# Half of a depthwise convolution as diagonal products on TensorE, and the query norm folded into the attention scores

## The reference

```
h = concat(meta, x)                                   # 272 x 1024
for l in range(2):
    z = rms(h) @ w_in[l]                              # 18 tiles of 128 columns
    ya = attention(z)    # 8 query heads, 2 key heads of 64; q, k rms-normed per head (gains q_norm_g, k_norm_g),
                         # s = q.k / 8 - slope * dist;  softmax with a sink;  chunks of 64, window 128, 16 meta keys
    yr = rwkv7(z)        # 4 heads; delta-rule recurrence, here in 5 chunks of 64
    yc = silu(layernorm(depthwise_conv31(z_a * sigmoid(z_b)) + conv_b))   # 256 channels, 31 taps, causal
    h = h + concat(ya, yr, yc) @ w_out[l]
    h = h + peer(rms(h))                              # product-key experts, 16384 experts a layer
```

## Time and profile before

| what | before |
|---|---|
| median of 3 runs | 2104.95 us (2094.97 to 2105.49) |
| the profiled execution's own time | 2105.58 us |
| its span | 2103.4 us |
| PE busy | 1977.3 us (94%) |
| DVE, ACT, POOL busy | 1459.2, 962.2, 1279.7 us |
| mean granted TensorE clock | 0.959 |
| mixer stage of layer 0 (end of projections to first `w_out` product) | 80.13 to 222.06 us |
| mixer stage of layer 1 | 1134.00 to 1278.23 us |

### The profile page before, as it was taken

How to read it: one execution, slowest core, us unless ns; L and a number is a source line. 1 busy time by engine, 2 the same in 40 slices (tenths; PEclk the granted TensorE clock), 3 DMA queues, 4 the chain that set the end, 5 groups by cost and what they waited for, 6 DMA issues and landing times.

```text
span 2103.4 us, 43605 instructions
## 1 busy us (share of the span) xinstructions
PE 1977.3 (94%) x16516; PEld 1889.8 (90%) x16516; DVE 1459.2 (69%) x2757; ACT 962.2 (46%) x1646; POOL 1279.7 (61%) x667
## 2 busy tenths in 40 slices
PE   9957999999999999999999577999999999999999
PEld 8845899999999999999988467999999999999998
DVE  3864419994777788788748535199627777887886
ACT  5422545554333455545554124455543333555553
POOL 5896469998666633233058964799976666332430
PEclk9966899999999999999999678999999999999999
DMA  5300356665444599899743002566555446998995
GB/s 188 102 1 1 92 170 189 181 180 170 151 143 147 180 339 313 288 313 315 249 135 106 1 1 82 179 192 186 183 169 151 145 146 202 349 322 303 323 328 158
DMA packets 106380, 387.80 MB, mean 184 GB/s; under 512 B 11808, under 2 KB 12064, under 8 KB 106016
## 3 DMA queue, kind: packets, MB, share of 16 engines
q1 hardware_dynamic: 87840, 319.25, 47.3%
q0 software_dynamic: 18432, 67.12, 9.2%
HBM read 385.27 MB, written 1.05 MB: 184 GB/s over the span
## 4 chain that ended last, share of the span: by engine, by line
PE 60%; POOL 24%; issue 13%; DVE 2%; ACT 1%; POOLq 0%; ACTq 0%
PE ps L895 60%; POOL w_lo L552 14%; POOL arena L568 6%; POOL arena L577 4%; DVE x L1386 0%; DVE x_lo L1379 0%; POOL arena L564 0%; ACT w_hi L635 0%; DVE onehots_j L1374 0%; DVE h L1816 0%; DVE sel L1702 0%; ACT L759 0%; ACT L610 0%; DVE h L1815 0%; DVE sel L1705 0%
## 5 line engine op out<-in xcount | busy, mean ns | idle before, releaser
L895 PE MATMUL ps<-x_hi,w_hi 128*128 128x240 f32 (+5 forms) x4768 | 1429.3, 324 | 20.4 <-POOL w_lo L552 10.7
L895 PE MATMUL ps<-x_hi,w_lo 128*128 128x240 f32 (+3 forms) x4768 | 1307.3, 274 | 0.0
L552 POOL TENSOR_TENSOR w_lo<-w,w_hi 128x1024 fp32r<-128x1024 f32 x346 | 871.3, 2536 | 390.6 <-ACT w_hi L635 390.0
L895 PEld LDWEIGHTS ps<-x_hi,w_hi 128*128 128x128 f32 x4768 | 904.2, 190 | 73.5 <-POOL w_lo L552 12.6
L895 PEld LDWEIGHTS ps<-x_hi,w_lo 128*128 128x128 f32 x4768 | 909.3, 191 | 0.0
L635 ACT CAST w_hi<-w 128x1024 fp32r<-128x1024 f32 x596 | 623.5, 1046 | 344.3 <-DMA w<-v_c 204.6
L895 PE MATMUL ps<-x_lo,w_hi 128*128 128x240 f32 (+3 forms) x2720 | 757.1, 278 | 0.0
L895 PEld LDWEIGHTS ps<-x_lo,w_hi 128*128 128x128 f32 x2720 | 519.0, 191 | 0.2
L1773 DVE TENSOR_TENSOR w_lo<-w,w_hi 128x1024 fp32r<-128x1024 f32 x250 | 305.6, 1222 | 114.5 <-ACT w_hi L635 113.7
L895 PE MATMUL ps<-arena 64*64 64x64 f32 (+9 forms) x2496 | 176.7, 277 | 60.9 <-ACT arena L783 19.7
L895 PEld LDWEIGHTS ps<-arena 64*64 64x64 f32 (+6 forms) x2496 | 152.0, 172 | 83.7 <-ACT arena L783 20.4
(11 more groups left out here) (187 smaller groups left out, 1691.7 us busy)
## 6 DMA issues: line engine op xcount, KB each, us to landing
w<-u_c SPq DMA_DIRECT2D x256, 512.0 KB, 3.6
w<-v_c SPq DMA_DIRECT2D x256, 512.0 KB, 5.5
w<-w_c SPq DMA_DIRECT2D x84, 512.0 KB, 3.6
arena<-keys_c SPq DMA_DIRECT2D x2, 1024.0 KB, 5.6
arena<-mix_c SPq DMA_DIRECT2D x2, 792.0 KB, 8.2
h<-h SPq DMA_DIRECT2D x2, 544.0 KB, 4.4
out<-x SPq DMA_DIRECT2D x4, 256.0 KB, 2.1
arena<-lora_c SPq DMA_DIRECT2D x2, 256.0 KB, 9.1
```

Source lines behind the costliest of these rows:

```text
L552: g.tensor_tensor(low_of(l, n, wlo_t), low_of(l, n, wraw_t), high_of(l, n).bitcast(F32), ALU.subtract).then_inc(s_lo, 1)
L895: return nc.tensor.matmul(out_, lhsT, rhs, start=start, stop=stop, skip_group_check=True)
```

## The change

Four things are changed, all in the mixer stage, in both layers.

1. Convolution: channels 128 to 255 (j = 1) go to PE. POOL makes 31 diagonal 128 x 128 matrices (the identity times the tap's weights) and PE adds up 31 fp32 products of 272 columns in PSUM bank 6, as fillers: `FILL` = 4 ahead of the inversion, 1 before each of the two `cm*ti` products of a level, 2 before each of the two next. ACT copies the sum with the bias. Channels 0 to 127 stay on POOL, with `tensor_scalar` always in its two-operation form. POOL's low halves of tiles 18 to 20 move behind the convolution.
2. Query norm: the raw query tiles go into the scores. The query's root mean square per token and head (24 columns) scales the distance term (`q_dist`) and the exponential (`q_exp`). Both gains go into the keys.
3. Squares of q and k, the value copies and the copies of transposed values move from DVE to ACT.
4. Attention steps start five calls earlier on PE, ACT and DVE. The transposes of the values stand with the sums of squares in PE's call 1. DVE's key norm stands in calls 2 and 3, between the masks of the last Gram matrices and the first `ti`.

```diff
+TAPS = (12, 6, 7, 6)
+CONV_BANK = 6
+UP_BANKS = (5, 4)
+FILL = (4, 1, 2)
...
+    put("slope", np.broadcast_to(np.tile(-np.array(SLOPES) * HD ** 0.5, NT), (P, NT * AH)))
...
@@ POOL
-                lows(l, 0 if l == 0 else AHEAD, NZ + AHEAD)
+                lows(l, 0 if l == 0 else AHEAD, NZ)
...
                 for k in range(CONV_K):
-                    for j in range(2):
-                        dst = cacc if k == 0 else ctmp
-                        ins = g.tensor_scalar(dst[:, j, :], cu[:, j, k:k + T], vcol(l, "conv_w", j * CONV_K + k),
-                                              vcol(l, "conv_b", j) if k == 0 else None, ALU.mult,
-                                              *((ALU.add,) if k == 0 else ()))
...
+                    g.tensor_scalar(tap(k), ident, vcol(l, "conv_w", CONV_K + k), 0.0, ALU.mult, ALU.add).then_inc(s_tap, 1)
+                for k in range(CONV_K):
+                    link(g.tensor_scalar((ctmp if k else cacc)[:, 0, :], cu[:, 0, k:k + T], vcol(l, "conv_w", k),
+                                         0.0 if k else vcol(l, "conv_b", 0), ALU.mult, ALU.add))
                     if k:
-                        ins = g.tensor_tensor(cacc[:, :, :], cacc[:, :, :], ctmp[:, :, :], ALU.add)
+                        ins = g.tensor_tensor(cacc[:, 0, :], cacc[:, 0, :], ctmp[:, 0, :], ALU.add)
-                lows(l, NZ + AHEAD, NP)
+                lows(l, NZ, NP)
@@ ACT
+            def evacuate_qk(l, n):      # used for tiles 12 to 16
+                high(l, n + AHEAD)
+                act.wait_ge(s_use, l * NW + n + 1)
+                nc.scalar.activation(sq[:, n - ZQ, :], ps[:, 1 + n % 2, 0:T], ACT.Square).then_inc(s_q2, 1)
+                nc.scalar.copy(z[:, n, 1:T + 1], ps[:, 1 + n % 2, 0:T]).then_inc(s_ea, 1)
...
+                root(qn, [(qn[:, 4, :], ps[:, K2_BANK, 0:T]), (q_rms, ps[:, Q2_BANK, 0:NT * AH])], 1.0 / HD,
                       res("norm_eps")).then_inc(s_qs, 1)
-                for _ in range(8):
+                act.wait_ge(s_vk, l + 1)
+                for s, (_, _, nk, (sl, b)) in enumerate(V_TILES):
+                    ins = nc.scalar.copy(vkey[0:nk, sl, b, :], ps[0:nk, V_BANKS[s % 2], (s // 2) * P:(s // 2 + 1) * P])
+                ins.then_inc(s_vkc, 1)
+                for _ in range(3):
                     yield
...
-                                                 scale=HD ** -0.5, accum_out=small[0:nq, 2, hh:hh + 1])
+                                                 scale=q_exp[0:nq, AH * s + hh:AH * s + hh + 1],
+                                                 accum_out=small[0:nq, 2, hh:hh + 1])
...     (after the inversion's copies, before WU)
+                act.wait_ge(s_cps, l + 1)
+                nc.scalar.activation(cacc[:, 1, :], ps[:, CONV_BANK, 0:T], ACT.Identity,
+                                     bias=vcol(l, "conv_b", 1)).then_inc(s_cpc, 1)
@@ PE
-                for c, (bank, at, t0, n) in enumerate(Q2_AT):
-                    last = mm(ps[:, bank, at:at + n], blk, sq[:, min(c, 4), t0:t0 + n], True, True)
+                mm(ps[:, K2_BANK, 0:T], blk, sq[:, NQK - 1, :], True, True)
+                for s in range(NT):
+                    q0 = TILES[s][0]
+                    for c in range(4):
+                        at = AH * s + c
+                        last = mm(ps[:, Q2_BANK, at:at + 5:4], sq[:, c, q0:q0 + P], blk[:, 0:P:HD], True, True)
                 last.then_inc(s_q2s, 1)
-                yield
-                for _ in range(7):
-                    yield
-                pe.wait_ge(s_qk, l + 1)
+                pe.wait_ge(s_vc, l + 1)
...     (the four transposes of the values)
+                for _ in range(4):
+                    yield
+                pe.wait_ge(s_qk, l + 1)
...
+            def convolution(l):
+                for k in range(CONV_K):
+                    pe.wait_ge(s_tap, CONV_K * l + k + 1)
+                    last = mm(ps[:, CONV_BANK, 0:T], tap(k), cu[:, 1, k:k + T], k == 0, k == CONV_K - 1)
+                    if k == CONV_K - 1:
+                        last.then_inc(s_cps, 1)
+                    yield
...     (ahead of the levels, and in each level)
+                for _ in range(FILL[0]):
+                    after(taps)
+                        for _ in range(FILL[1]):
+                            after(taps)
                         pe.wait_ge(s_ti, 2 * nlev * l + 2 * b + j + 1)
...
+                        for _ in range(FILL[2]):
+                            after(taps)
                         pe.wait_ge(s_xc, 2 * nlev * l + 2 * b + j + 1)
...
+                pe.wait_ge(s_cpc, l + 1)
@@ DVE
-                for c in range(0, 5, 2):
-                    a = qn[:, c:min(c + 2, 5), :]
-                    link(v.reciprocal(a, a))
-                    yield
-                for c in range(5):
-                    link(v.scalar_tensor_tensor(qn[:, c, :], z[:, ZQ + c, 1:T + 1], vcol(l, "kg" if c == 4 else "qg"),
-                                                qn[:, c, :], ALU.mult, ALU.mult))
...
+                yield
+                dve.wait_ge(s_qs, l + 1)
+                link(v.reciprocal(qn[:, 4, :], qn[:, 4, :]))
+                link(v.tensor_tensor(gain, vcol(l, "qg"), vcol(l, "kg"), ALU.mult))
+                link(v.tensor_scalar(q_exp, q_rms, HD ** 0.5, None, ALU.mult))
+                link(v.reciprocal(q_exp, q_exp))
+                link(v.tensor_tensor(q_dist, q_rms, mix("slope"), ALU.mult))
+                yield
+                link(v.scalar_tensor_tensor(qn[:, 4, :], z[:, ZK, 1:T + 1], gain, qn[:, 4, :], ALU.mult, ALU.mult))
+                link(v.tensor_copy(kcat[:, 0:NMETA], qn[:, 4, 0:NMETA]))
+                v.tensor_copy(kcat[:, NMETA:208], qn[:, 4, 80:T]).then_inc(s_qk, 1)
...
-                    link(v.scalar_tensor_tensor(m_, m_, HD ** -0.5, sink, ALU.mult, ALU.max))
+                    link(v.tensor_tensor(m_, m_, q_exp[0:nq, AH * s:AH * (s + 1)], ALU.mult))
+                    link(v.tensor_tensor(m_, m_, sink, ALU.max))
...
-                v.tensor_tensor(sq[:, 0:5, :], z[:, ZQ:ZQ + 5, 1:T + 1], z[:, ZQ:ZQ + 5, 1:T + 1],
-                                ALU.mult).then_inc(s_q2, 1)
```

More of the change, by code:

```diff
@@ L284, in trunk, with tap @@
         ident, ones, iota, fold = res("ident"), res("ones"), res("iota"), res("fold")
+        def tap(k):
+            t, i = tap_at[k]
+            return t[:, i * P:(i + 1) * P]
         def vcol(l, name, i=0, parts=slice(0, P)):
@@ L313, in trunk @@
         t1, t2, t3 = two(), two(), two(TP)
+        q_rms, q_dist, q_exp = (A.take(NT * AH) for _ in range(3))
+        gain = A.take(1)
         over = A.at
@@ L329, in trunk @@
         cm = A.take(2 * TP).rearrange("p (j c t) -> p j c t", j=2, c=NCH)
+        tap_t = (A.take(TAPS[0] * P), sel_t[:, NR:NR + TAPS[1] * P], ohA_t[:, 0:TAPS[2] * P], ohB_t[:, 0:TAPS[3] * P])
+        tap_at = [(t, i) for t, n in zip(tap_t, TAPS) for i in range(n)]
         A.at = over + 6 * T
@@ L439, in trunk @@
         s_qs = sem("qk_scale_ready")
-        s_qk = sem("qk_normed")
+        s_qk = sem("keys_normed_and_query_scales_ready")
+        s_vc = sem("last_keys_v_copied")
         s_vk = sem("keys_v_in_psum")
@@ L464, in trunk @@
         s_conv = sem("conv_done")
+        s_tap = sem("conv_tap_matrices_ready")
+        s_cps = sem("conv_second_block_in_psum")
+        s_cpc = sem("conv_second_block_copied")
         s_gl = sem("pool_link")
@@ L662, in evacuate, with evacuate_v @@
                 nc.scalar.copy(dst, ps[:, 1 + n % 2, 0:nt]).then_inc(s_ea, 1)
+            def evacuate_qk(l, n):
[3 more added lines that the diff above has]
+                nc.scalar.copy(z[:, n, 1:T + 1], ps[:, 1 + n % 2, 0:T]).then_inc(s_ea, 1)
+            def evacuate_v(l, n):
+                high(l, n + AHEAD)
+                act.wait_ge(s_use, l * NW + n + 1)
+                nc.scalar.copy(vcat[:, 0:NMETA], ps[:, 1 + n % 2, 0:NMETA])
+                nc.scalar.copy(vcat[:, NMETA:208], ps[:, 1 + n % 2, 80:T]).then_inc(s_vc, 1)
+                nc.scalar.copy(z[:, n, 1:T + 1], ps[:, 1 + n % 2, 0:T]).then_inc(s_ea, 1)
             def evacuate_stay(l, n):
@@ L677, in attention @@
                 act.wait_ge(s_q2s, l + 1)
-                root(qn, [(qn[:, min(c, 4), t0:t0 + n], ps[:, bank, at:at + n])
-                           for c, (bank, at, t0, n) in enumerate(Q2_AT)], 1.0 / HD,
+                root(qn, [(qn[:, 4, :], ps[:, K2_BANK, 0:T]), (q_rms, ps[:, Q2_BANK, 0:NT * AH])], 1.0 / HD,
                       res("norm_eps")).then_inc(s_qs, 1)
-                for _ in range(8):
+                act.wait_ge(s_vk, l + 1)
[3 more added lines that the diff above has]
+                for _ in range(3):
                     yield
@@ L761, in _ @@
                 nc.scalar.activation(dexc[:, :, :], lw[:, :, :], ACT.Exp).then_inc(s_ad, 1)
-                for n in range(13, NZ):
-                    evacuate(l, n, z[:, n, 1:T + 1], T)
+                for n in range(ZQ + 1, ZV):
```

(17 more changed lines are left out.)

42 lines of the change are left out of this document (13 added, 29 removed).

## The result

The change took 2107.28 us (median of 20 runs, 2105.11 to 2112.2), the kernel before 2103.09 on the same chip. The ratio is 1.0026, with a 95% interval of 1.0016 to 1.0035. A second set of runs gave 1.0044 [1.0028, 1.0060]. So the change is slower by 0.2 to 0.6% (5.5 us by the first ratio, 9.2 by the second), where 17 us of gain were forecast. The profiled execution took 2107.25 us, its span is 2105.4.

What follows compares the result with a forecast made beforehand. It took engines waiting in turn in the inversion, not POOL's convolution, as the bound. Layer 0 at -6 and layer 1 at -11 gave -17 from 2105.6, or 2088.6, stated as 2088 us against the median; range 2066 to 2108.

Steps and rivals of the forecast that it cites:

- the +1.5: Stretch behind layer 0's inversion: cost in us of DVE's maximum and normalisation now standing before `carry`.
- +7 in the inversion: Each layer's inversion: 7 us lost because PE's granted clock would average about 0.88 instead of full.
- rival 4: POOL's convolution is on the path after all, taking over 100 us instead of 55; chance under 1 in 100.
- The +3 for DVE: Layer 0's inversion: small DVE operations held by POOL's low halves, 3 us (0 to 8.4).
- +4.5 forecast: Start of each layer's mixer: -0.7 + 1.2 + 3.9 = +4.4 us, +4.5 with the end of ACT's copies.
- the +1.2: Start of the mixer, PE: sums of squares and value transposes take 3.9 us against 2.7 (-0.2 to 1.5).
- 78 forecast: Layer 1's inversion: 53 work + 14 waits + 4 turnaround + 7 clock = 78 us, against 90.7 before.
- rival 2: Inversions: TensorE becomes the bound at half clock, deciding from a mean clock of about 0.76; 2130 us; chance 0.1.
- -8.5: Stretch behind layer 0's inversion: 8.5 us shorter, as attention steps leave it, after paying 1.5 before `carry`.
- rival 3: End of layer 0: queue order makes `carry` pay about 8 us more and the tail stays longer; about 2098; chance 0.2.
- Rival 1: Inversions: TensorE keeps full clock, so the clock's +7 a layer and the +3 go; 2071 us; chance 0.2.
- three signs of being wrong: Start longer by 8, inversion clock under 0.75, or layer 0's last attention step again the last thing before `w_out`.

Runs made afterwards that it cites:

- e2: The kernel before with only POOL's convolution tensor_scalar put in the two-operation form; 2107.24 us, ratio 1.0024.
- e1: The change with both halves of the convolution on POOL in the two-operation form, no products on PE; 2102.96 us, ratio 1.002.
- e5: e4 with the keys' sum and DVE's key norm ahead of the Gram masks, and no fillers ahead of the levels; 2098.24 us, ratio 0.9992.
- e3: The change with constants instead of per-partition operands in the exponentials and distance reads, leaving out the query's root mean square; 2100.26 us, ratio 1.0004.
- e9: The change with layer 0's third-tile normalisation and transposes two calls later, ACT's step one later; 2098.93 us, ratio 1.0001.
- e10: e8 with e9's move of the third tile's steps in layer 0; 2066.47 us, ratio 0.9854.
- e7: The change with the 31 convolution products on PE placed in runs ahead of waits known from the trace; 2092.74 us, ratio 0.9961.
- e8: The change with the moves of e4, e5 and e7 together: late query sums, early key norm, products in the waits; 2073.17 us, ratio 0.9880.
- e6: e8 with both convolution halves on POOL, no products on PE; 2087.02 us, ratio 0.9955.
- e4: The change with the query's sums of squares, root and small DVE operations moved from the start into the inversion; 2110.37 us, ratio 1.0042.

## Why the prediction was wrong

The sum failed mainly at its term for the stretch behind layer 0's inversion (the +1.5) and at its term for the clock (+7 in the inversion, nothing in the start). The parts follow.

**What bounds the kernel** was right: e2 and e1 both show that POOL's convolution isn't on the path, and rival 4 fell at once. POOL went as forecast:
```profile
84.20 2.47 POOL L585 TENSOR_SCALAR onehots_i<-res,vecs 128x128 f32<-128x128 f32 x7
...
90.86 0.50 POOL L587 TENSOR_SCALAR arena<-arena,vecs 128x272 f32<-128x272 f32 x1
...
133.69 0.77 POOL L590 TENSOR_TENSOR arena<-arena 128x272 f32<-128x272 f32 x1
134.41 6.96 POOL L571 TENSOR_TENSOR w_lo<-w,w_hi 128x1024 fp32r<-128x1024 f32 x3
```
Matrices ready at 88.8 (forecast 88), last add at 134.5 (133), low halves until 141.4 (141). The +3 for DVE held by those low halves didn't come: the first maximum of that time fell behind them, at 145.5. The prediction also read only one side of the earlier trace rows. DVE kept its 0.51 beside `tensor_scalar`, but the two `tensor_scalar` beside it took 2.34 where the earlier trace rows has 1.91:
```profile
97.25 2.34 POOL L568 TENSOR_SCALAR arena<-arena,vecs 128x272 f32<-128x272 f32 x2
```
So there it was POOL that gave way. In the change its taps took 0.61 for 0.50 beside DVE's updates from 103.98 to 110.65; POOL has room for that.

**Start of the mixer** (+4.5 forecast, +7.6 and +6.3 measured). PE's work rose by 1.7 and 1.9, near the +1.2. Its idle time rose by 2.0 and 2.1 where the key norm less the 0.7 came to 3.2: the key norm without its three small operations costs 1.8 to 2.4 (e5). The failed term is the clock, which the prediction put at nothing here and which took 3.9 and 2.3. The narrow products cost what was said, but not what follows them: 2.5 us of this on the Gram matrices of layer 0 (8.26 for 5.75), 1.6 in layer 1.

**Inversion, layer 1** (78 forecast, 86.4 measured). The work is 57.0 (busy time times clock) for 53, which is 4 short. Most of that is the length of the products: from start to start, times clock, the 64 x 64 ones take about 22.5 for 19.8, and the convolution's 17.9 for 16.7. The idle time is 16.3 for 18, counting the 14 of waits and the 4 of turnaround, which are time between engines. What failed is the clock: it cost 13.0 instead of 7, at a mean of 0.83 where 0.88 was taken. That is on the way to rival 2, short of its 0.76. The waits:
```profile
PE ps L932 <- ACT arena L816: 8.6, 2, 4.6
PE ps L932 <- DVE arena L1494: 4.4, 2, 2.3
PE ps L1021 <- DVE arena L1511: 2.3, 2, 1.8
```
These are 2.1 and 2.3 for the first scores (at and over the upper estimate), and 4.0 and 4.6 behind exponentials that e3 shows to be longer by their pointer operands. *Layer 0* came out at 75.2 for 75 by luck, from errors that cancel: idle 13.1 (13 + 3), work at full clock 51.4 (49), clock 10.6 (7), and nothing for the low halves beside DVE (3).

**Behind the inversion.** Layer 1 went further than forecast (-5.9 for -3). Layer 0 is the largest single error: +0.9 for -8.5. The step that failed is the +1.5 for DVE's maximum and normalisation "before `carry`". What stands in the state chain isn't DVE's two operations but the whole passage from maximum over ACT's exponentials to the normalised probabilities: PE idles 4.8 at the transposes, which are ahead of the chain's next products in its own list, and the stretch runs at a clock of 0.68 for 0.81. PE's idle time in it rose by 6.3 (1.3 to 7.7), its clock cost by 1.5 (5.1 to 6.6), and its work fell by 6.9, where the prediction took away 10. The mechanism is the chain of rival 3, priced there at 8; 9.4 came. Its other half, the longer tail, didn't. e9 and e10 took 6.2 and 5.3 out of the stretch by moving the normalisation and the transposes two calls, with the maximum left in its place.

**Tails.** Layer 0 -8.7 (-7.5), layer 1 -0.9 (0): right.

**The sum.** Forecast -17, measured +2.0 in span. The difference of 19 is: starts 4.9, inversions 0.2 and 8.3, the stretch behind layer 0's 9.4 less 2.9 in layer 1, tails -2.1; the rest, some 1 us, is rounding (the -6 of layer 0 was -5 by its own terms) and lies outside the mixers. I had treated rivals 2 and 3 and the start as alternatives; they all came in part. Rival 1, a full clock, did not. None of the three signs of being wrong showed: the starts were longer by 7.6 and not 8, the clock was 0.83 and not under 0.75, and the last wait before `w_out` was for DVE's closing norms. They were set too wide. The measured 2107.3 lies just inside the range's end of 2108.

## What to carry to other kernels

Place filler products directly ahead of a wait that is known from the trace, in a row and not one by one; spread evenly, the same 31 products here cost what they filled (e1), and moved into the waits they gained (e7, e8 against e5, e6). When attention steps are moved in front of a recurrence, count the whole round trip over the other engines as a wait in the recurrence, unless the step that consumes it is moved back past it. Price every operand that turns from an immediate into a pointer, and look at the granted clock behind narrow products. Split a stretch into work, idle time and clock cost before and after a move: here a saving in one stretch came back as clock in the next (e4).

## What the runs showed of the hardware

- The 24 fp32 instructions of 2 columns, 0.12 us each with PE busy throughout, were followed by a fall of the granted clock from 1.00 to 0.50 (2.4 to 1.2 GHz) in ten of twelve starts; without them it held to the Gram matrices' end in all ten starts of e4, e5, e8, e6 and e10 (0.99 to 1.00 over e4's starts).
- `tensor_scalar` on POOL: 0.50 us in the two-operation form for 272 columns against 0.96 in the one-operation form of the earlier trace rows, for the same product, and 0.61 beside DVE's updates.
- A tensor_scalar of 128 columns in the two-operation form takes 0.35 us on POOL (2.47 for seven).
- A per-partition scale adds 0.094 us to ACT's exponential, a per-partition scalar 0.06 us to DVE's scalar_tensor_tensor, at 144 and at 208 columns alike.
